# One opening stage for the first norm, the constants, the loads by token tile and the bias table, with late weight pieces asked for by the input stage

## The reference, cut to what matters

```python
def rms_norm(x, g):
    xf = x.astype(jnp.float32)
    y = xf * lax.rsqrt(jnp.mean(jnp.square(xf), axis=-1, keepdims=True) + EPS)
    return (y * g.astype(jnp.float32)).astype(x.dtype)

# even block, first steps
h = rms_norm(x, ev_mix_norm)          # (512, 1024)
proj = h @ ev_w_in                    # (1024, 1720): q, k, v, gates, latents
bias = rel_bias[t5_bucket(distance)]  # (heads, distances), a table of 32 buckets
```

## Time and profile before

| | us |
|---|---|
| median of 3 runs | 2542.63 (2537.89 to 2549.76) |
| the profiled execution | 2534.28 |
| its span in the profile | 2531.6 |
| busy: PE, PEld | 2150.8 (85%), 1636.9 (65%) |
| busy: DVE, ACT, POOL | 1329.5 (53%), 982.4 (39%), 194.2 (8%) |
| first operation of the input stage `ev_in` | 50.23 |

### The profile page before, as it was taken

One profiled execution on the slowest core, in us unless ns is written; L12 is line 12 of the kernel. 1 busy time (PEld: TensorE's weight loads), 2 busy tenths in 40 slices (PEclk: granted clock), 3 DMA queues, 4 the chain that ended last, 5 costly groups with the idle time before them and its releaser, 6 DMA issues. The chain is left out here.

```text
span 2531.6 us, 34168 instructions
## 1 busy us (share of the span) xinstructions
PE 2150.8 (85%) x12764; PEld 1636.9 (65%) x12764; DVE 1329.5 (53%) x1910; ACT 982.4 (39%) x1259; POOL 194.2 (8%) x208
## 2 busy tenths in 40 slices
PE   3958689789999989995999999994997777686995
PEld 3737343468888877875888888883574367375774
DVE  1351774643333224434666666664467676234886
ACT  2121563733222222123555556653254500123874
POOL 0010000000000000002000100012021200002011
PEclk7975898989999999996999999997998879586998
DMA  6100600123133125004777787785210000116996
GB/s 180 49 17 1 226 33 17 67 75 104 54 117 117 50 83 183 1 34 157 277 274 283 273 282 271 284 282 189 62 68 11 1 1 2 67 59 177 363 376 255
DMA packets 223537, 343.25 MB, mean 136 GB/s; under 512 B 50909, under 2 KB 135805, under 8 KB 223438
## 3 DMA queue, kind: packets, MB, share of 16 engines
q1 hardware_dynamic: 215006, 318.73, 37.2%
q0 software_dynamic: 8432, 23.23, 2.6%
HBM read 312.46 MB, written 28.39 MB: 135 GB/s over the span
## 5 line engine op out<-in xcount | busy, mean ns | idle before, releaser
L1388 DVE TENSOR_TENSOR moe_pass_wL<-moe_pass_w,moe_pass_wH 128x2048 fp32r<-128x2048 f32 (+1 forms) x146 | 308.2, 2115 | 152.4 <-ACT moe_pass_wH L1330 152.3
L1330 ACT ACTIVATE moe_pass_wH<-moe_pass_w 128x2048 fp32r<-128x2048 f32 (+1 forms) x146 | 258.6, 1777 | 141.3 <-PE PS L549 110.6
L1388 DVE TENSOR_TENSOR hm_pass_wL<-hm_pass_w,hm_pass_wH 128x2048 fp32r<-128x2048 f32 x62 | 140.2, 2286 | 40.0 <-ACT hm_pass_wH L1330 39.9
L547 PE MATMUL PS<-moe_pass_wL,moe_pass_xgH 128*128 128x512 f32 (+1 forms) x384 | 148.7, 387 | 3.5 <-DVE moe_pass_xgL L1393 3.5
L547 PE MATMUL PS<-xnT_low,ffn_upH 128*128 128x512 f32 x352 | 140.0, 398 | 5.7 <-DVE xnT_low L863 5.4
L548 PE MATMUL PS<-moe_pass_wH,moe_pass_xgL 128*128 128x512 f32 (+1 forms) x384 | 143.2, 373 | 0.0
L549 PE MATMUL PS<-moe_pass_wH,moe_pass_xgH 128*128 128x512 f32 (+1 forms) x384 | 143.2, 373 | 0.0
L549 PE MATMUL PS<-ffn_xH,ffn_upH 128*128 128x512 f32 x352 | 139.1, 395 | 0.0
L548 PE MATMUL PS<-ffn_xH,ffn_up_low 128*128 128x512 f32 x352 | 138.1, 392 | 0.0
L1330 ACT ACTIVATE hm_pass_wH<-hm_pass_w 128x2048 fp32r<-128x2048 f32 x62 | 116.8, 1912 | 19.4 <-PEq L1246 5.8
L870 DVE TENSOR_TENSOR ffn_hT<-ffn_sg,PS 128x512 f32<-128x512 f32 x22 | 15.2, 689 | 167.3 <-PE PS L549 167.3
(11 more groups left out here) (773 smaller groups left out, 5082.0 us busy)
## 6 DMA issues: line engine op xcount, KB each, us to landing
moe_pass_w<-in_moe_w_down SPq DMA_DIRECT2D x40, 1024.0 KB, 4.9
moe_pass_w<-in_moe_w_gate SPq DMA_DIRECT2D x34, 1024.0 KB, 5.9
moe_pass_w<-in_moe_w_up SPq DMA_DIRECT2D x32, 1024.0 KB, 6.1
hm_pass_w<-in_exp_w_gate SPq DMA_DIRECT2D x44, 512.0 KB, 6.2
hm_pass_w<-in_exp_w_up SPq DMA_DIRECT2D x40, 512.0 KB, 6.7
hm_pass_w<-in_exp_w_down SPq DMA_DIRECT2D x40, 512.0 KB, 5.9
od_W<-in_od_w_in SPq DMA_DIRECT2D x12, 1024.0 KB, 10.8
moe_pass_w<-in_moe_w_gate SPq DMA_DIRECT2D x16, 768.0 KB, 4.5
```

What stands on the lines that cost most here:

```text
L547: nc.tensor.matmul(out, lh, rl, start=start, stop=False)
L1330: nc.scalar.activation(wH[:, i % S, 0:n], w[:, i % R, 0:n], ACT.Copy).then_inc(s["high"], 1)
L1388: nc.vector.tensor_tensor(wL[:, i % S, 0:n], w[:, i % R, 0:n], f32(wH[:, i % S, 0:n]), ALU.subtract) \
```

## The change

The first five stages become one, called `start`; `load_weights` is split between it and `load_rest`.

- SP: x is asked for in four transfers, one for each token tile, each with its own semaphore. The bucket table, `rel_bias` and the row of ones are asked for after the second. Then `gx`, pieces 2, 3 and 4 of W, the three gain vectors. Last SP waits until DVE has copied the bias table, and asks for the write to the scratch tensor.
- POOL: the identity first (its last step signals `ident`), then the other constants, then `X` and `vblk`.
- ACT and DVE: the norm as before, but each square waits for its own tile. DVE takes two of the three bias copies (`keep(0)`, `keep(1)`) between the mean and the reciprocal, and the third after the reciprocal. It waits for `gx` before the gain products.
- PE: the three bias matmuls first, into banks 5 to 7, then the transposes; ahead of those of tile 2 it waits for the three copies, as their banks are reused.
- `by_head` gets a tile of its own, 6 KB in each of 8 partitions.
- SP in the input stage: 16 transfers of piece 0 and piece 1, then a wait for the scratch write and the 8 reads of `TcT`, and then the small vectors and the compression weights as before.

```diff
-    with stage(nc, "consts", "zeroed") as (block, s):
-        @block.sync
-        def _(sp):
-            for i, n in enumerate(("ev_ffn_norm", "od_mix_norm", "norm1_g_2")):
...
-                def load_weights(sp):
-                    sp.dma_start(E, D["bucket_table"]).then_inc(loaded["tables"], 16)
-                    sp.dma_start(relb[0:BUCKETS, :], D["rel_bias"]).then_inc(loaded["tables"], 16)
-                    sp.dma_start(relb[BUCKETS:BUCKETS + 1, :], D["ones_row"]).then_inc(loaded["tables"], 16)
-                    for i in (2, 3, 4):
-                        a, b = pieces[i]
-                        sp.dma_start(W[:, :, a:b], win[:, :, a:b]).then_inc(loaded[f"w{i}"], 16)
-
+                scratch = nc.dram_tensor("bias_by_distance", [NH, 3 * SEQ], F32, kind="Internal").ap()
+
+                def load_rest(sp):
+                    nonlocal small
                     for i in range(2):
                         dst = W[:, :, 0:KC0].rearrange("p k (j s d) -> p k j s d", s=2, d=HD)[:, :, :, i]
                         for k in range(KD):
@@ -1628,9 +1607,10 @@
                                 .then_inc(loaded["w0"], 16)
                     a, b = pieces[1]
                     sp.dma_start(W[:, :, a:b], win[:, :, a:b]).then_inc(loaded["w1"], 16)
-
-                def load_rest(sp):
-                    nonlocal small
+                    sp.wait_ge(loaded["scratch"], 16)
+                    for h in range(NH):
+                        src = bass.AP(scratch.tensor, h * 3 * SEQ + SEQ + FWD_ZERO - (CMP_L - 1) - 31 * CMP_S, [[CMP_S, 32], [1, SEQ]])
+                        sp.dma_start(TcT[h % 4 * 32:h % 4 * 32 + 32, h // 4], src).then_inc(loaded["bias"], 16)
...
-                with stage(nc, "ev_load", "zeroed") as (block, s):
+                xs = yT[:, :, :].rearrange("p (t a) b -> p t (a b)", a=2)
+                with ExitStack() as m0, stage(nc, "start", "zeroed ident squared_a squared_v mean root rstd scaled turned made copied") as (block, s):
+                    ss = sb("ss", [P, 4, NT], m0)
+                    PS = C.PS
+
                     @block.sync
                     def _(sp):
+                        for t in range(NT):
+                            sp.dma_start(x[:, t], D["x"][0, t * P:(t + 1) * P]).then_inc(loaded[f"x{t}"], 16)
+                            if t == 1:
+                                sp.dma_start(E, D["bucket_table"]).then_inc(loaded["tables"], 16)
+                                sp.dma_start(relb[0:BUCKETS, :], D["rel_bias"]).then_inc(loaded["tables"], 16)
+                                sp.dma_start(relb[BUCKETS:BUCKETS + 1, :], D["ones_row"]).then_inc(loaded["tables"], 16)
                         sp.dma_start(gx[:, :], D["ev_mix_norm"][0].rearrange("(p k) -> p k", k=KD)).then_inc(loaded["gx"], 16)
-                        sp.dma_start(x[:, :, :], D["x"][0].rearrange("(t p) d -> p t d", p=P)).then_inc(loaded["x"], 16)
-                        sp.wait_ge(loaded["x"], 16)
+                        for i in (2, 3, 4):
+                            a, b = pieces[i]
+                            sp.dma_start(W[:, :, a:b], win[:, :, a:b]).then_inc(loaded[f"w{i}"], 16)
+                        for i, n in enumerate(("ev_ffn_norm", "od_mix_norm", "norm1_g_2")):
+                            sp.dma_start(C.gains[:, i], D[n][0].rearrange("(p k) -> p k", k=KD)).then_inc(C.gains_come, 16)
+                        sp.wait_ge(s["copied"], 3)
+                        sp.dma_start(scratch, by_head[:, :, :].rearrange("p a b -> p (a b)")).then_inc(loaded["scratch"], 16)
 
                     @block.gpsimd
                     def _(pool):
                         step = Steps(pool, s["zeroed"])
+                        step(nc.gpsimd.memset(C.ident[:, :], 0.0))
+                        nc.gpsimd.affine_select(out=C.ident[:, :], in_=C.ident[:, :], compare_op=ALU.not_equal, fill=1.0,
+                                                base=0, pattern=[[-1, P]], channel_multiplier=1).then_inc(s["ident"], 1)
+                        pool.wait_ge(s["ident"], 1)
+                        for tile, value in ((C.ones, 1.0), (C.one, 1.0), (C.causal, 0.0), (C.ones64, 0.0)):
+                            step(nc.gpsimd.memset(tile[:, :], value))
+                        for a in (0, 64):
+                            step(nc.gpsimd.memset(C.ones64[a:a + 64, a:a + 64], 1.0))
+                        step(nc.gpsimd.affine_select(out=C.causal[:, :], in_=C.causal[:, :], compare_op=ALU.is_ge, fill=NEG,
+                                                     base=0, pattern=[[-1, P]], channel_multiplier=1))
                         step(nc.gpsimd.memset(X[:, :, :, :, :], 0.0))
                         step(nc.gpsimd.memset(vblk[:, :, :, :], 0.0))
 
-                with stage(nc, "ev_wait", "x") as (block, s):
+                    @block.scalar
+                    def _(act):
+                        for t in (0, 1):
+                            act.wait_ge(loaded[f"x{t}"], 16)
+                            nc.scalar.activation(xs[:, t], x[:, t], ACT.Square, accum_out=ss[:, 0, t:t + 1]).then_inc(s["squared_a"], 1)
+                        act.wait_ge(s["mean"], 1)
+                        nc.scalar.activation(ss[:, 2], ss[:, 1], ACT.Sqrt).then_inc(s["root"], 1)
+                        act.wait_ge(s["rstd"], 1)
+                        for t in range(NT):
+                            nc.scalar.activation(xs[:, t], x[:, t], ACT.Copy, scale=ss[:, 3, t:t + 1]).then_inc(s["scaled"], 1)
+
                     @block.vector
                     def _(dve):
+                        for t in (2, 3):
+                            dve.wait_ge(loaded[f"x{t}"], 16)
+                            nc.vector.tensor_tensor_reduce(out=xs[:, t], in0=x[:, t], in1=x[:, t], scale=1.0, scalar=0.0, op0=ALU.mult,
+                                                           op1=ALU.add, accum_out=ss[:, 0, t:t + 1]).then_inc(s["squared_v"], 1)
+                        dve.wait_ge(s["squared_a"], 2)
+                        dve.wait_ge(s["squared_v"], 2)
+                        nc.vector.tensor_scalar(ss[:, 1], ss[:, 0], 1.0 / DM, EPS, ALU.mult, ALU.add).then_inc(s["mean"], 1)
+
+                        def keep(i):
+                            dve.wait_ge(s["made"], i + 1)
+                            nc.vector.tensor_copy(by_head[:, i], PS[0:NH, 5 + i, :]).then_inc(s["copied"], 1)
+
+                        keep(0)
+                        keep(1)
+                        dve.wait_ge(s["root"], 1)
+                        nc.vector.reciprocal(ss[:, 3], ss[:, 2]).then_inc(s["rstd"], 1)
+                        keep(2)
                         dve.wait_ge(loaded["gx"], 16)
-                        dve.wait_ge(loaded["x"], 16)
-
-                norm_transpose(nc, C, x, gx, xnT, yT[:, :, :].rearrange("p (t a) b -> p t (a b)", a=2), "ev_norm", load_weights)
-
-
-
-
-
-                scratch = nc.dram_tensor("bias_by_distance", [NH, 3 * SEQ], F32, kind="Internal").ap()
-                with stage(nc, "ev_bias", "made copied") as (block, s):
-                    PS = C.PS
-                    by_head = cq6[0:NH, 0:3]
+                        for t in range(NT):
+                            dve.wait_ge(s["turned"], t + 1)
+                            for h in range(2):
+                                g = bcast(gx[:, 4 * h:4 * h + 4].unsqueeze(2), [P, 4, P])
+                                nc.vector.tensor_tensor(xnT[:, 4 * h:4 * h + 4, t * P:(t + 1) * P],
+                                                        PS[:, 2 * t + h].rearrange("p (k c) -> p k c", k=4), g, ALU.mult)
 
                     @block.tensor
                     def _(pe):
                         pe.wait_ge(loaded["tables"], 48)
                         for i in range(3):
-                            nc.tensor.matmul(PS[0:NH, i, :], relb[:, :], E[:, i * SEQ:(i + 1) * SEQ], start=True, stop=True) \
-                                .then_inc(s["made"], 1)
-
-                    @block.vector
-                    def _(dve):
-                        dve.wait_ge(s["made"], 3)
-                        for i in range(3):
-                            ins = nc.vector.tensor_copy(by_head[:, i], PS[0:NH, i, :])
-                        ins.then_inc(s["copied"], 1)
-
-                    @block.sync
-                    def _(sp):
-                        sp.wait_ge(s["copied"], 1)
-                        sp.dma_start(scratch, by_head.rearrange("p a b -> p (a b)")).then_inc(loaded["scratch"], 16)
-                        sp.wait_ge(loaded["scratch"], 16)
-                        for h in range(NH):
-                            src = bass.AP(scratch.tensor, h * 3 * SEQ + SEQ + FWD_ZERO - (CMP_L - 1) - 31 * CMP_S, [[CMP_S, 32], [1, SEQ]])
-                            sp.dma_start(TcT[h % 4 * 32:h % 4 * 32 + 32, h // 4], src).then_inc(loaded["bias"], 16)
-
```

(33 more changed lines are left out.)

## The result

The changed kernel takes 2511.31 us (median of 4 runs, 2505.49 to 2516.52), the kernel before 2546.2 (median of 4, 2537.89 to 2550.73). The ratio (time after through time before) is 0.9876, 95% interval 0.9846 to 0.9906: 1.2% faster. The prediction was 2511.6. It was a saving of 31.0 us taken off 2542.63, the median of the first three of these four runs of before; the medians of all four runs each are 34.9 us apart.

The account below looks back on a forecast made before the run. Serial opening stages, held up by x's load and SP's issues, were taken to bound the opening. Savings of 28.1 (earlier input stage) and 2.9 (clock) sum to 31.0: 2542.63 to 2511.6 us; range 2511.6 less 8 to 2524.

Parts of the forecast that it names:

- What bounds the opening: Opening: a sum of barrier-separated stages, held up by x landing at 12.49 and SP issuing piece 0 until 34.74 us.
- Start of the input stage: End of the opening: the input stage starts at 22.1 in place of 50.23, 28.1 us saved.
- the last tile at 9.3: Loads of x: last tile lands at 9.3 us, from 1.03 first issue, 7.8 transfer and 0.5 for the table.
- The copies: DVE between mean and reciprocal: two bias copies of 0.63 us each, about 1.0 us on the chain.
- The root's table load stands ahead of the wait: ACT in the norm: its 1.28 us load comes before the wait for the mean, over by 9.3.
- The tables at 7: Bias work: tables land at about 7 us, good side 4.7, bad side 19; PE waits at most 7 us.
- The price of lateness: Opening rival: each microsecond tables land after about 7 delays the whole norm; at 19, 2523.6 us; chance 0.07.
- SP's new list: SP in the opening: gains issued by 9, then a wait for the third bias copy; ends at about 14, not last.
- The late pieces cost nothing: Input stage: piece 0 issued by 39, landed by about 42, needed at about 72; cover 30 us, cost nothing.
- The clock, 2.9 us: Start of the input stage: PE's clock stays at 1.00 over a 2.5 us gap, saving 2.9 us.
- a clock of 1.00 at the start: Sign of being right, at the input stage's start: PE's clock at 1.00 there.
- first rival: PE's clock falls in the gap before the input stage or never rose: 28.1 saved, 2514.5 us; chance 0.32.

Follow-up runs that it names:

- e2: Kernel before with only weight pieces 0 and 1 asked for in the input stage, all opening stages kept; ratio to the kernel before 0.9942.
- e3: Changed kernel with weight pieces 0 and 1 asked for in the opening again, behind pieces 2 to 4; ratio to the kernel before 0.9922.
- e10: Changed kernel with x asked for in one transfer, the tables behind it, all squares waiting for it; ratio to the kernel before 0.9886.
- e4: Changed kernel with the bucket table, rel_bias and row of ones asked for behind pieces 2 to 4; ratio to the kernel before 0.9942.
- e13: Changed kernel run again with nothing edited, beside the version with both edits; ratio to the kernel before 0.9873.

## Why the prediction held, point by point

- **What bounds the opening.** SP's issues of piece 0 and the serial stages: e2 and e3 give each its share by the profiles, 8.9 us for the late pieces and 19.5 for the one stage. Within the 19.5 only the loads by tile were taken alone (e10, 2 us); how the rest divides between the bias chain, the two stages that only waited for loads, and the stage ends no run shows.
- **Start of the input stage: 22.1 forecast, 21.97 to 22.98 measured.** The saving up to there is 27.25 in place of 28.1 in the first pair of profiles. x: the forecast has the last tile at 9.3, and so, at its 1.28 a tile, tile 2 at 8.0. Tile 2 was there at 8.92, DVE's two squares ran one behind the other, and the mean was done at 11.75 in place of 10.8. The sum had put the table ahead of tile 2 at 0.5 us, for its bytes; e4 prices the three small loads there at 1.7 (tile 2 at 7.19), 1.4 of which is SP's time to issue them. The copies cost 0.8 us where the sum had 1.0 to 1.3, the tail from the first scaling to the last product 9.17 (13.04 to 22.21) where it had 8.82.
- **The root's table load stands ahead of the wait:** it started at 8.03, before the mean at 11.58. In e10, where the squares ended late, it ran from 11.56 to 12.84, past the mean at 12.0, and still the copies were last.
- **The tables at 7:** 7.9, beyond the 7 us of wait that the prediction gave as a sign, and no harm from it: the first copy follows the mean at once. The price of lateness, one microsecond of start for each microsecond, was right: in e4 they came 12.8 later and the stage started 12.1 later.
- **SP's new list:** last issue at 14.28 (about 14 forecast), in part by luck. The gains were to be issued by 9, with a wait for the third copy behind them. Pieces 2 to 4 took 5.47 us to issue and the first gain vector 3.04, so the gains were done at 14.23; the third copy had ended at 13.92.
- **The late pieces cost nothing:** the sixth job's operation is at 74.62, 5.54 behind the fifth, as before (5.53). Right, with more cover (time between landing and use) than given: piece 0 is issued in 9.8 us.
- **The clock, 2.9 us: the term that was off.** The first profile gave 1.2 (6.99 to 5.80), e13 gave the 2.8 in full. The prediction's sign for it, a clock of 1.00 at the start, was seen in e13 and not in the two others (0.58 and 0.59 over the first 4 us). The forecast and its first rival were put as two cases of the kernel. One profile shows the forecast's outcome, two show one between it and the rival's, and none the rival's in full. The transposes do bring the clock up: in the kernel before PE had done nothing until its first transpose at 20.75, and single ones go from 421 ns at first to 273 at the end. The rule of the Trainium skill that was weighed in the prediction (TensorE: Matmul & The Clock Gate, Part 4: PE-mode transpose) is contradicted by this too. In the changed kernel the bias matmuls end 1.1 us ahead of the transposes, so there they can have a part in the rise.
- **The median, 2511.6 against 2511.31,** is closer than the steps deserve, and that is luck. The forecast of 31.0 was taken off a median of 2542.63; up to the end of the input stage the profiles show 28.4, in one execution 31.2, and the four-run medians 34.9. The profiled execution came out 9.2 us above its forecast, since the one it was taken off was a short one of before. The kernel before was 2542 to 2546 in its later medians, the changed one 2511 to 2514.

## What to carry to other kernels

Where every stage ends in a barrier, look for the engine that ends each stage's list, and count the issuing of loads as work: SP held up two stages here while all compute engines were idle, and moving its issues to the next stage, where they have cover, cost nothing. Put small tables that open a second chain behind the first data that the first chain needs, and not behind large pieces; but count their issues too, as here they held back the next tile by 1.7 us. And compare the stretch that was changed, not the spans of one execution each: the untouched rest of this kernel varies by 17 us over 14 profiles, more than half of the whole gain.

## What the runs showed of the hardware that was not expected

The same 16 transfers take SP 16.53 us to issue right behind 3.9 MB of queued loads (16.50 in e3), 11.81 behind 4.2 MB of compression weights (e7), and 9.1 to 10.0 when the loads ahead have landed. A small load asked for behind large ones took far longer: the first gain vector was issued for 3.04 us and landed 10.0 us after its issue in the changed kernel, where the same transfer took 1.7 in the kernel before. And whether TensorE's clock falls around a gap of 2.2 to 2.7 us differs between executions of one program: it was at full speed over the input stage's first 4 us in one profile of three, behind the longest of the gaps (2.72), and at a mean of 0.58 or 0.59 in the other two, where it fell only after the products had begun.
